# First products of the compressed attention branch: operands exchanged, four column groups in turn

## What is computed

```
def compress_blocks(t, pe, w1, w2):
    n_cmp = (s - CMP_BLOCK) // CMP_STRIDE + 1          # 15
    idx = np.arange(n_cmp)[:, None] * CMP_STRIDE + np.arange(CMP_BLOCK)[None, :]
    blk = jnp.swapaxes(t[:, idx], 2, 3) + pe
    blk = blk.reshape(b, n_cmp, hk, CMP_BLOCK * d)
    return jax.nn.gelu(blk @ w1) @ w2
```

## Time and profile before

| | |
|---|---|
| median of three runs | 2363.6 us |
| the profiled execution's own time | 2363.92 us |
| its span, first to last instruction | 2362.6 us |
| PE busy | 2322.3 us, 98% |
| DVE busy, ACT busy | 1367.0 us, 1158.6 us |
| first products (L675) | 128 records, 15.6 us busy, from 1163.2 to 1207.2 |
| TensorE's granted clock, mean | 0.997 |

### The profile page before, as it was taken

The page is one execution under the profiler, slowest core; times in us unless marked ns, Lnnn a source line. Parts: engine busy times, 40 slices in busy tenths (PEclk is TensorE's granted clock), DMA queues, the critical chain, the costliest instruction groups (busy, mean ns, idle before and its releaser), DMA issues.

```text
span 2362.6 us, 27386 instructions
## 1 busy us (share of the span) xinstructions
PE 2322.3 (98%) x11188; PEld 1921.5 (81%) x11188; DVE 1367.0 (58%) x1930; ACT 1158.6 (49%) x1635; POOL 9.6 (0%) x17
## 2 busy tenths in 40 slices
PE   8999999999999999999999999999999999999997
PEld 6788788888788888888888887888888888888886
DVE  5676555656555577687666555645545544544554
ACT  5456654556654564453445455445444344434443
POOL 0000000000000000000000000000000000000000
PEclk9999999999999999999999999999999999999999
DMA  7454445564545553333554455555565565555552
GB/s 260 132 177 153 143 154 188 174 196 143 162 159 196 161 166 107 125 126 107 166 191 143 157 164 178 178 196 193 181 195 181 194 192 184 194 184 191 195 179 107
DMA packets 204269, 400.10 MB, mean 169 GB/s; under 512 B 12656, under 2 KB 12816, under 8 KB 203760
## 3 DMA queue, kind: packets, MB, share of 16 engines
q1 hardware_dynamic: 201920, 391.08, 50.3%
q0 software_dynamic: 1648, 6.32, 1.0%
q10 hardware_dynamic: 576, 0.95, 0.1%
HBM read 396.23 MB, written 2.10 MB: 169 GB/s over the span
## 4 chain that ended last, share of the span: by engine, by line
PE 93%; DVE 3%; ACT 2%; issue 1%; DMA 0%; SPq 0%; DVEq 0%; ACTq 0%
PE ACC L795 28%; PE ACC L797 27%; PE ACC L796 27%; PE TP L428 2%; ACT arena L818 1%; PE PV L629 1%; PE SC L624 1%; DVE WL L1673 1%; PE PV L632 1%; PE SC L465 1%; PE TP L473 1%; PE SC L675 1%; PE PV L483 0%; PE PV L482 0%; PE PV L481 0%
## 5 line engine op out<-in xcount | busy, mean ns | idle before, releaser
L1673 DVE TENSOR_TENSOR WL<-W,WH 128x1024 fp32r<-128x1024 f32 x740 | 900.8, 1219 | 656.0 <-ACT WH L818 654.3
L818 ACT ACTIVATE WH<-W 128x1024 fp32r<-128x1024 f32 x740 | 781.3, 1056 | 839.6 <-PE ACC L797 835.3
L795 PE MATMUL ACC<-WH,XH 128*128 128x512 f32 x2592 | 1045.7, 403 | 7.0 <-ACT arena L818 4.8
L797 PE MATMUL ACC<-WH,XL 128*128 128x512 f32 x2592 | 1013.5, 391 | 0.0
L796 PE MATMUL ACC<-WL,XH 128*128 128x512 f32 x2592 | 1011.7, 390 | 0.0
L795 PEld LDWEIGHTS ACC<-WH,XH 128*128 128x128 f32 x2592 | 488.1, 188 | 116.8 <-issue 15.2
L797 PEld LDWEIGHTS ACC<-WH,XL 128*128 128x128 f32 x2592 | 487.4, 188 | 105.9
L796 PEld LDWEIGHTS ACC<-WL,XH 128*128 128x128 f32 x2592 | 488.7, 189 | 92.1 <-issue 1.0
L795 PE MATMUL ACC<-WH,HH 128*128 128x512 f32 x352 | 139.3, 396 | 0.0
L797 PE MATMUL ACC<-WH,HL 128*128 128x512 f32 x352 | 137.8, 392 | 0.0
L796 PE MATMUL ACC<-WL,HH 128*128 128x512 f32 x352 | 137.6, 391 | 0.0
(11 more groups left out here) (255 smaller groups left out, 1414.2 us busy)
## 6 DMA issues: line engine op xcount, KB each, us to landing
W<-in_w_in SPq DMA_DIRECT2D x84, 1024.0 KB, 4.9
W<-in_a_w_in SPq DMA_DIRECT2D x48, 1024.0 KB, 5.1
W<-in_w_ffn_gate SPq DMA_DIRECT2D x44, 1024.0 KB, 5.2
W<-in_w_ffn_up SPq DMA_DIRECT2D x44, 1024.0 KB, 5.2
W<-in_w_ffn_down SPq DMA_DIRECT2D x44, 1024.0 KB, 5.1
W<-in_b_w_in SPq DMA_DIRECT2D x40, 1024.0 KB, 5.1
W<-in_a_w_out SPq DMA_DIRECT2D x16, 1024.0 KB, 5.0
W<-in_b_w_out SPq DMA_DIRECT2D x16, 1024.0 KB, 5.1
```

Source lines behind the costliest of these rows:

```text
L795: MM(out, hx, WH[:, k, 0:ch.width], start=q == 0 and k == 0, stop=False)
L797: ins = MM(out, lx, WH[:, k, 0:ch.width], start=False, stop=last and k == QK - 1)
L818: return nc.scalar.activation(out, in_, func, **how)
L1673: TT(tiles_of(M.WL[n % 2], ch, half), tiles_of(M.W[n % 4], ch, half), tiles_of(M.WH[n % 2], ch, half).bitcast(F32), ALU.subtract).then_inc ...
```

## The change

The two operands exchange places. The blocks, padded with zeros from 30 to 32 columns (`PADC`), are now loaded, and the matrix `M.W1[:, n, :]` is streamed, 128 columns. The result is blocks by hidden numbers, 32 x 128, and it goes to one of four strips of 32 partitions of the bank `SC[j]`, taken in turn (n % 4); so the array's four groups of 32 columns are used one after the other, and each strip holds the sum of eight of the 32 positions. Sixteen matmuls, in place of eight, are issued in a visit, over two visits in place of four.

ACT then copies the bank, 128 x 128, to `M.HT[j]`. One more matmul on PE adds the four quarters and turns the result back at once: it loads `M.HT[j]` and streams `M.quarters`, 128 x 30, which holds for each block four ones, at its place in each strip; the result, 128 x 30, goes to bank `TP[j]`. The Gelu reads from there. DVE makes the zeros of the padding and `M.quarters` (a reduction over the identity) ahead of its four L1567 at j = 0. `compressed` and `nsa_attend` start two visits later.

```diff
@@ side_plan
-    begin(after("c.kv2") + 29, "compressed")
+    begin(after("c.kv2") + 31, "compressed")
...
-        begin(after("c.nq1") + 2 + 50 * g, "nsa_attend", g)
+        begin(after("c.nq1") + 4 + 50 * g, "nsa_attend", g)
@@ memory
-    M.W1, M.BL = cut(4096, 32, HD), cut(8192, 32, 2 * NC2)
+    M.HT, M.quarters = [cut(i * HD, HD) for i in range(2)], cut(2 * HD, 2 * NC2)
+    M.W1, M.BL = cut(4096, 32, HD), cut(8192, 32, PADC)
@@ pe_program, compress
-            ins = MM(SC[j][:, 0:2 * NC2], M.W1[:, n, :], M.BL[:, n, :], start=n == 0, stop=n == 31)
-            if n % 8 == 7:
+
+            rows = slice(PADC * (n % 4), PADC * (n % 4 + 1))
+            ins = MM(SC[j][rows, 0:HD], M.BL[:, n, :], M.W1[:, n, :], start=n < 4, stop=n >= 28)
+            if n % 16 == 15:
                 if n == 31:
                     ins.then_inc(*did("hidden_multiplied", j))
                 yield
-        emptied[f"SC{j}"] = ("hidden_activated", j)
+        emptied[f"SC{j}"] = ("hidden_taken", j)
+        yield
+        yield
+        wait_empty(f"TP{j}")
+        pe.wait_ge(*at("hidden_taken", j))
+        pe.wait_ge(*at("quarters_stacked"))
+        MM(TP[j][:, 0:2 * NC2], M.HT[j], M.quarters, start=True, stop=True).then_inc(*did("hidden_summed", j))
+        emptied[f"TP{j}"] = ("hidden_activated", j)
+        yield
@@ act_program, compress
-        for _ in range(6):
+        for _ in range(4):
             yield
         act.wait_ge(*at("hidden_multiplied", j))
-        A(M.H1[j], SC[j][:, 0:2 * NC2], ACT.Gelu_apprx_tanh).then_inc(*did("hidden_activated", j))
+        A(M.HT[j], SC[j][:, 0:HD], ACT.Copy).then_inc(*did("hidden_taken", j))
+        yield
+        yield
+        yield
+        act.wait_ge(*at("hidden_summed", j))
+        A(M.H1[j], TP[j][:, 0:2 * NC2], ACT.Gelu_apprx_tanh).then_inc(*did("hidden_activated", j))
         yield
@@ dve_program, compress
         dve.wait_ge(*at("compress_weights_landed"))
+        if j == 0:
+            V.memset(M.BL[:, :, 2 * NC2:PADC], 0.0)
+            V.tensor_reduce(M.quarters, M.ident.rearrange("p (j c) -> p c j", j=4)[:, 0:2 * NC2, :], AX.X, ALU.add).then_inc(*did("quarters_stacked"))
         if j == 1:
```

## The result

The changed kernel takes 2353.12 us (median of 5 runs, 2352.71 to 2353.72). The kernel before, run beside it, takes 2363.6 us (5 runs, 2360.28 to 2369.82). The ratio over all runs is 0.9939, with an interval of 0.9917 to 0.996; the medians differ by 10.5 us (0.9956), where I had predicted 3.0. The profiled execution took 2353.72 us, its span 2352.4.

A forecast was written before the change was run, and what follows sets the result against it. The prediction took TensorE (PE), busy 98% of the span, as the bound. Its terms, -14.3 + 9.0 + 1.3 + 0.45 + 0.35 = -3.2 us, gave 2360.7 from 2363.9 or 2360.4 from the median; it said 2360.6, range 2355.3 to 2367.0.

The forecast's parts named there:

- removed: On PE's path: the old products' 128 records at 0.112 us each go away, -14.3 us.
- new products and array division: On PE: 64 exchanged matmuls at 0.14 us, +9.0 us; entering and leaving column strips in four visits, +1.3 us.
- sums of the quarters: On PE: two added matmuls, four records at 0.112 us, +0.45 us.
- DVE ahead of the first product: At j = 0, DVE's memset and reduction ahead of L1567 lengthen PE's idle wait, +0.35 us.
- clock: Behind PE's idle gap: the 3.42 us at 0.50 clock stay in both kernels, 0 us, bounds 1.7 either way.
- The step that failed: In the new products: a matmul's two records share a group, so only pairs overlap, 9.0 us; chance 0.45.
- the right case among the rivals: In the new products: all four groups stream at once, 27 ns a record, -8.4 us, 2355.5; chance 0.20.
- no overlap at all: In the new products: streams follow each other through one array, +1.6 us, 2365.5, or 2368.9 with bare loads; chance 0.22.
- a drain at each change of group: In the new products: each matmul pays 0.10 us of drain and a 27 ns load, +9.6 us, 2373.5; chance 0.06.
- the signs of being wrong: In the changed profile: record pace under 0.04 or over 0.13 us, paired records not blocking, or several 0.50-clock stretches near 1165.
- The case of the vanished drop together with all groups at once: Full overlap plus a vanished clock drop: a little more chance of being faster than 2356.5, in all 0.12.
- The term put at nothing: In compressed and nsa_attend: starting two visits later keeps the distances between them, 0 us, bounds of 0.5 either way.

The follow-up runs named there:

- e1: The changed kernel with eight matmuls in a row going to the same strip (n // 8): median 2362.21 us, ratio to before 0.9981.
- e7: The changed kernel with all 32 matmuls of a j in one visit in place of two: median 2353.7 us, ratio to before 0.995.
- e2: The changed kernel with the strip changing after every second matmul (n // 2 % 4): median 2353.18 us, ratio to before 0.9944.
- e11: The changed kernel with the strip changing after every fourth matmul (n // 4 % 4): median 2358.88 us, ratio to before 0.9971.
- e3: The changed kernel with only two strips by turns in a visit: median 2356.68 us, ratio to before 0.9961.
- e6: The kernel before with the products of j = 0 and the Gelu two visits later: median 2360.09 us, ratio to before 0.9977.
- e4: The kernel before with its 30-column products issued sixteen matmuls a visit in place of eight: median 2373.47 us, ratio to before 1.0031.
- e9: The changed kernel unchanged, run and profiled once more: median 2353.68 us, ratio to before 0.9943.
- e5: The changed kernel with the products of j = 0, the copy and the Gelu two visits later: median 2351.75 us, ratio 0.9944.

## Why the prediction was wrong

The kernel came out 7.5 us below my 2360.6 and 2.2 us below the range. By the terms of the sum, measured between neighbours in the two timelines (streamed matmuls otherwise start 0.227 us apart):

| term | predicted us | measured us | from |
|---|---|---|---|
| removed | -14.3 | -14.4 | 8 blocks of 1.81: 1171.73 to 1173.99 is 2.26, less 2 x 0.227 |
| new products and array division | +9.0 and +1.3 | +4.9 | 4 visits of 1.22: L808 at 1189.59 to L807 at 1191.26 is 1.67, less 2 x 0.227 |
| sums of the quarters | +0.45 | +0.45 | 2 of 0.226: 1171.64 to 1172.32 is 0.68, less 2 x 0.227 |
| DVE ahead of the first product | +0.35 | +0.27 | the wait is 2.23 in place of 1.96 |
| clock | 0 | -1.7 | 3.42 us at half clock are gone |
| sum | -3.2 | -10.5 | the local stretch has -10.9 |
| behind the local stretch | 0 | +0.8 | 1129.4 in place of 1128.6 to the span's end; the span has -10.2 |

**Right**: that PE's own stream is what counts; the price of the removed records, 0.112 us, by starts and not by durations; that the load sets the pace before and the stream after, 0.83 to 0.84 ns a column for both, so that turning alone wins next to nothing (e1); the loads of 32 columns, predicted at 107 ns, now 106 to 110 in duration; the entry, whose first load stands 0.3 us behind L808, and the way out with its bare load (e7: 0.32 us a visit for 0.33); the sums; ACT's copy, which made PE wait nowhere. In the loads' timeline of after the bare entry and the bare load of L700 behind the block are seen:

```profile
1166.27 0.81 PEld L678 LDWEIGHTS SC<-arena 128*32 128x32 f32 x32 [0.35 <-issue]
1167.28 0.42 PEld L700 LDWEIGHTS TP<-consts,arena 128*128 128x128 f32 x4 [0.20 <-issue]
```

**The small term of DVE** was right in kind. The memset and the reduction overlap in the record (they start at 1160.97 and 1160.99), so it came to 0.27 rather than 0.35:

```profile
1158.65 2.36 DVE L1692 TENSOR_TENSOR WL<-W,WH 128x1024 fp32r<-128x1024 f32 x2
1160.97 0.11 DVE L1577 MEMSET arena<- 128x64 f32 x1
1160.99 0.29 DVE L1578 TENSOR_REDUCE arena<-consts 128x30 f32<-128x120 f32 x1
1161.20 1.95 DVE L1586 TENSOR_TENSOR arena<-arena 128x240 f32<-128x240 f32 x4
```

**The step that failed** is this one: "The second cannot stream before the first has streamed its 128 columns, 107 ns; only then can the next group's first record join." The first half is true, the second isn't. The second record of a matmul does wait for its strip, but the next strip's record goes past it; it takes about four records on a strip before the next is held up (e2, e11, e1). The starts show both halves. In e11, where eight records in a row go to one strip, the first two records of the first block cover 0.38 us, of which the last takes 0.27 to 0.30: they start about 0.1 us apart. In after the first four records cover 0.32 us, so all four start within 0.05 us of each other:

```profile
1162.81 0.38 PE L679 MATMUL SC<-arena 128*32 128x128 f32 x2 [2.23 <-DVE arena L1587]
...
1163.30 0.32 PE L678 MATMUL SC<-arena 128*32 128x128 f32 x4 [2.23 <-DVE arena L1586]
```

A row stands in order of its start and does not name its strip. But two records of one strip start 0.109 us apart, so the four of after are the first records of the four strips, and the second records, issued between them, start behind them.

Of the nine microseconds that I put in for the products, 5.4 were this assumption: 9.0 + 1.3 against 4.9. I had the right case among the rivals, worked out to 3.5 + 0.3 + 1.3 = 5.1 us (measured 4.9), and gave it 0.20. Its number was met by luck, though. I had taken 27 ns a record as the load of 32 columns or the smallest distance of issue, "the smallest distance seen". e3 has the same loads and the same issue and takes twice as long, so the 0.027 us are four streams of 0.109 side by side, and the starts of after come closer than 27 ns: four within 0.05 us. What held the case down was the argument that two records of one matmul share a group. It was my argument and no row's.

The 0.027 us of the earlier trace rows are no price of an issue either. Those first two records of a block stand behind streamed matmuls. Behind the idle gap the first two start about 0.1 us apart (0.38 us less the last one's 0.27 to 0.28), as all later ones do:

```profile
1163.18 0.38 PE L675 MATMUL SC<-arena 128*128 128x30 f32 x2 [1.96 <-DVE arena L1567]
```

That fits a load that was already done while a 512-column matmul streamed (0.227 us), which leaves the 30 streamed columns, 25 ns at 0.84 each. No run was made to test this reading.

Two of the other rivals are settled as well: with no overlap at all a block would have taken 3.5 us, and with a drain at each change of group the kernel would have been at 2373.5. After changes the group at every matmul and takes 1.01 us a block. Of the signs of being wrong that I had named, the first came: a pace under 0.04 us.

The Trainium skill bears on this twice. Its page "TensorE: Matmul & The Clock Gate", section "The mechanism", says that a load overlaps running matmuls only where the row group differs. Here all four strips use the same 128 rows and differ by columns, and in after 32 loads of 106 to 110 ns cover 0.81 us while the matmuls run: the trace does not agree. The same page's section "Measured speedup vs the span model" gives 2.38 times for three column tiles of 512 columns; the four here give 4.0 times at 128 fp32 columns (0.109 to 0.027 us a record, without entry and exit), a better pace than the 0.045 us that I had estimated from it.

**The clock term** failed too. I saw the low stretch and kept it, because the idle gap ahead of it stays. But e6 (no gap) and the seven profiles with a gap of 2.2 us and products that stream 128 columns all run there at 1.00, and e4 gets 13.65 us at 1.2 GHz with no gap ahead. My bound of 1.7 us was the right size and the value that I took was not; what I left out of the account was what PE does in the microseconds behind the gap, and that the same gap need not bring the low clock each time (e9 and after near 39 us). The case of the vanished drop together with all groups at once was in the text ("a little more if a clock drop vanishes"), but not in the range, which ended at one of the two.

**The term put at nothing.** The starts of `compressed` and `nsa_attend` two visits later were to cost 0, with bounds of 0.5 either way. Behind the local stretch the kernel after takes 0.8 us more, some 0.5 of it at L474's new wait for ACT. I had looked only at the waits that the kernel before had.

**What stays open.** The runs of the kernel before lie in groups, near 2360.2, 2363.5, 2369.7 and 2372 to 2374 us (17 to 22 runs beside each set of experiments), with a lower mean clock in the longer ones (0.997 to 0.998, 0.996 to 0.997, 0.993 to 0.994, and 0.992 to 0.993), while after has all of its own 11 runs within 3.1 us. The profiled runs of before are of the second group; where the others have their low clock was not profiled. The first group, 11 of the 61 runs, lies 3.3 us below the second. By an estimate from 1.7 us for each stretch of 3.4 us at half clock, two such stretches are missing in it, so the one near 1165 is probably not in every run of before. e6 has none of the groups above 2361.1 in 12 runs, which makes the gap together with the 30-column products likely as the cause of the longer ones; this is argued and not shown. Also open are 0.3 of the 0.8 us behind the local stretch, 0.1 of the 0.6 us of e5, and the 0.4 us between the local sum and its terms.

## What to carry to other kernels

Where an fp32 product loads 128 columns of weights and streams few, give the small operand to the load and spread the sum over column groups: what a single group can't win, four by turns win fourfold, and one matmul adds the quarters back. Cost such a thing by streams per group, and change the group at least every two fp32 matmuls. A term that is kept "equal" in both kernels, as a stretch at the low clock, deserves its own question: what was the engine doing there, does it still do that, and is the stretch there in a second execution. A task that is moved by two visits can meet another engine at a worse moment; look at the waits behind the change for names that were not there before.

## What the hardware showed that I had not expected

- Four column groups of 32 stream fp32 fully side by side: 0.027 us a record against 0.109 for one group, over 32 and over 64 records.
- A group takes about four records before it holds up those behind: changing after two takes 1.01 us for 32 records, after four 1.05, after eight 2.36, after sixteen 3.18. Two records of one group start 0.109 us apart, and each is about 273 ns long in the trace, whether 30 or 128 columns are streamed.
- The clock fell to 1.2 GHz for 13.65 us behind a 3.5 us block of products that each load 128 columns and stream 30, back to back with its neighbours; the same arithmetic as 128-column streams on 32-column loads left it at 2.4 GHz in nine profiles of nine, in seven of them behind 2.2 us of idle time.
- The same wait of 1.9 us ahead of the same streamed matmuls, near 39 us, was followed by 3.41 us at 1.2 GHz in e9 and by full clock in after, the same kernel: an idle gap of this length did not decide it by itself.
